# Staggering the starts of eight weight buffers by 64 bytes each

## The reference

```python
for l in range(DEPTH):
    h = rms_norm(x, pre_mix_g[l])
    mix = parallel_mixer(h, positions, w_in[l], ...)
    x = x + rms_norm(mix, post_mix_g[l])
    h = rms_norm(x, pre_cross_g[l])
    x = x + rms_norm(memory_cross_attention(h, mem_n, ...), post_cross_g[l])
    h = rms_norm(x, pre_ffn_g[l])
    x = x + rms_norm(swiglu(h, w_gate[l], w_up[l], w_down[l]), post_ffn_g[l])
```

## Time and profile before

| what | value |
|---|---|
| time, median of 3 runs | 2247.41 us |
| the three runs | 2243.59, 2257.13, 2247.41 us |
| span of the profiled execution | 2240.2 us |
| PE busy | 2145.6 us, 96% |
| DVE busy | 1403.7 us, 63% |
| ACT busy | 1127.0 us, 50% |
| POOL busy | 72.4 us, 3% |
| mean granted TensorE clock | 0.983 |

### The profile page before, as it was taken

One profiled execution on the slowest core, in us unless ns is written; L12 is line 12 of the kernel. 1 busy time (PEld: TensorE's weight loads), 2 busy tenths in 40 slices (PEclk: granted clock), 3 DMA queues, 4 the chain that ended last, 5 costly groups with the idle time before them and its releaser, 6 DMA issues.

```text
span 2240.2 us, 40831 instructions
## 1 busy us (share of the span) xinstructions
PE 2145.6 (96%) x17446; PEld 2047.7 (91%) x17446; DVE 1403.7 (63%) x2152; ACT 1127.0 (50%) x1757; POOL 72.4 (3%) x80
## 2 busy tenths in 40 slices
PE   7979999999989999999999999999999999999999
PEld 6868899989868899999998888999999998889999
DVE  5755566656646566566568667665666666668664
ACT  4554444444735444454546555545444456556443
POOL 4100000000000000000000000000000000000000
PEclk9989999999989999999999999999999989999999
DMA  6433346746415265645655224566566553335654
GB/s 216 151 113 104 106 150 212 217 145 194 135 51 167 90 190 196 205 163 191 205 186 171 95 95 142 184 192 205 180 195 203 174 170 114 95 114 168 198 195 155
DMA packets 98485, 360.33 MB, mean 161 GB/s; under 512 B 11136, under 2 KB 11149, under 8 KB 97920
## 3 DMA queue, kind: packets, MB, share of 16 engines
q1 hardware_dynamic: 96192, 349.22, 47.8%
q0 software_dynamic: 1680, 5.35, 0.8%
q10 hardware_dynamic: 432, 3.15, 0.4%
HBM read 356.61 MB, written 3.43 MB: 161 GB/s over the span
## 4 chain that ended last, share of the span: by engine, by line
PE 81%; DVE 12%; ACT 5%; issue 1%; DMA 0%; DVEq 0%; ACTq 0%; SPq 0%
PE bank L296 71%; DVE w_lo L1437 3%; PE bank L408 2%; ACT w_hi L907 1%; DVE rinv L1828 1%; PE bank L413 1%; PE bank L409 1%; PE bank L322 1%; DVE xn_lo L1459 1%; PE bank L759 1%; DVE sq L1499 1%; DVE x L1503 1%; DVE sq L2015 1%; DVE scale L1477 0%; DMA raw<-in_stream 0%
## 5 line engine op out<-in xcount | busy, mean ns | idle before, releaser
L1437 DVE TENSOR_TENSOR w_lo<-raw,w_hi 128x1024 fp32r<-128x1024 f32 x664 | 793.8, 1232 | 381.2 <-ACT w_hi L907 380.8
L296 PE MATMUL bank<-xn_hi,w_hi 128*128 128x256 f32 x3168 | 892.2, 282 | 38.3 <-DVE xn_lo L1459 30.2
L296 PE MATMUL bank<-xn_lo,w_hi 128*128 128x256 f32 x3168 | 880.5, 278 | 0.0
L296 PE MATMUL bank<-xn_hi,w_lo 128*128 128x256 f32 x3168 | 880.4, 278 | 0.0
L907 ACT ACTIVATE w_hi<-raw 128x1024 fp32r<-128x1024 f32 x664 | 672.2, 1050 | 231.6 <-PE bank L296 209.9
L296 PEld LDWEIGHTS bank<-xn_hi,w_hi 128*128 128x128 f32 x3168 | 598.4, 189 | 51.2 <-issue 25.8
L296 PEld LDWEIGHTS bank<-xn_lo,w_hi 128*128 128x128 f32 x3168 | 598.4, 189 | 1.3 <-issue 1.0
L296 PEld LDWEIGHTS bank<-xn_hi,w_lo 128*128 128x128 f32 x3168 | 598.0, 189 | 0.0
L296 PE MATMUL bank<-hid_hi,w_lo 128*128 128x256 f32 x1056 | 291.5, 276 | 0.0
L296 PE MATMUL bank<-hid_hi,w_hi 128*128 128x256 f32 x1056 | 291.5, 276 | 0.0
L296 PE MATMUL bank<-hid_lo,w_hi 128*128 128x256 f32 x1056 | 291.5, 276 | 0.0
(11 more groups left out here) (354 smaller groups left out, 2758.1 us busy)
## 6 DMA issues: line engine op xcount, KB each, us to landing
raw<-in_stream SPq DMA_DIRECT2D x664, 512.0 KB, 4.2
skew<-vec POOLq DMA_DIRECT2D x12, 192.0 KB, 4.2
table<-skew POOLq DMA_DIRECT2D x1, 1408.0 KB, 7.2
con<-in_con ACTq DMA_DIRECT2D x1, 1029.0 KB, 15.0
x<-in_x ACTq DMA_DIRECT2D x1, 1024.0 KB, 6.8
xn<-in_mem ACTq DMA_DIRECT2D x1, 1024.0 KB, 11.5
out<-x SPq DMA_DIRECT2D x4, 256.0 KB, 3.4
logit<-in_small POOLq DMA_DIRECT2D x3, 288.5 KB, 3.1
```

Source lines behind the costliest of these rows:

```text
L296: m = T.matmul(out, a, b, start=first and j == 0, stop=True, skip_group_check=True)
L1437: V.tensor_tensor(w_lo[m % RING], raw[m % RING], w_hi[m % RING].bitcast(F32), ALU.subtract).then_inc(*lo_done.next())
```

## The change

The buffers of `raw` stay where they are. Between each two of the eight buffers of `w_hi` and `w_lo` lies a new unused tile of 64 bytes, seven in all.

```diff
-    w_hi = [sb(f"w_hi{r}", [P, HK, COLS], F32R) for r in range(RING)]
-    w_lo = [sb(f"w_lo{r}", [P, HK, COLS], F32R) for r in range(RING)]
+    w_hi, w_lo = [], []
+    for part, ring in (("hi", w_hi), ("lo", w_lo)):
+        for r in range(RING):
+            if ring or part == "lo":
+                sb(f"offset_{part}{r}", [P, 16])
+            ring.append(sb(f"w_{part}{r}", [P, HK, COLS], F32R))
```

## The result

The changed kernel took 2285.7 us in the median of four runs (2283.99 to 2287.09), the kernel before 2251.14 us in its four. The ratio is 1.0168, with a 95% interval of 1.0131 to 1.0205. The forecast was no change at 2247 us; the time lies inside the stated range and in the case that had a chance of 0.25.

The account below looks back on a forecast made before the run. TensorE, busy 96% of the span, was taken as the bound, with matmul pitch the large lever. All five parts summed to 0, so the 2240.2 us span plus 7.2 us carried to the median gave 2247 us, range 2222 to 2298.

Parts of the forecast that it names:

- the case that had a chance of 0.25: The slow matmul pitch spreads through the feed-forward stretches: 2270 to 2298 us, chance 0.25.
- Part one: TensorE's matmul pitch: address distance alone does not set it, so taken as 0, bounds -13.6 to +50.7 us.
- The slower rival: Weights' load beside streamed activation read: a distance of 0 spreads the slow pitch, +50.7 us, 2298 us; chance 0.25.
- The faster rival: TensorE's two reads: stagger removes a standing clash, pitch falls to 109.2 ns, 73 us saved, 2174 us; chance 0.18.
- The case that the change does nothing: Unused tiles in the allocation could be dropped or padded away; called unlikely, time 2247 us, within the 0.57 for no effect.
- Parts two to five: w_lo on VectorE, w_hi on ScalarE, loads into raw, and tiles behind the rings moved by 448 bytes: each taken as 0.

Follow-up runs that it names:

- e1: Against the kernel before, only the tiles behind the rings moved up by 448 bytes, all weight buffers staying at byte 192: 2246.75 us, ratio 0.9994.
- e3: Against e1, all four w_lo buffers moved to byte 448, 256 from their w_hi, without a stagger: 2247.11 us, ratio 0.999 to before.
- e5: Against e1, everything from the shared area on, activations and weight buffers alike, moved 448 bytes higher: two runs, 2230.01 and 2265.8 us.
- e13: Against e1, only raw moved, to byte 256, weights staying at distance 64 from the activations: 2246.64 us, ratio 0.9971 to before.
- e7_both_128: Against e1, all w_hi and w_lo buffers moved to byte 256, distance 128 from the activations: 2301.07 us.
- e2_both_512: Against e1, all eight weight buffers moved to byte 640, distance 512 from the activations, no stagger: 2312.44 us, ratio 1.0294 to before.

## Why the prediction was wrong

**Part one, the matmul pitch, is the step that failed**, and nearly all of the 44.5 us with it. I took 0 where it was +42.9 us in the networks. The reason given was that four distances (64, 576, -64 and 448 bytes modulo 1 KB) "allow the fast pitch". Modulo 256 these are 64, 64, 192 and 192: two values, and the only two of the ten tried at which the fast pitch was found. The closing sentence named this hole, "a pitch that depends on the distance in a way that four distances happen to miss", and the range was wide enough for it, but the chance was set by the count of four. The change took w_hi to 64, 128, 192 and 256. The uniform kernels have 113.3 or 117.8, 118.7 or 120.0, 117.8, and 120.0 there; the changed kernel's four places have 113.6 or 117.9, 118.2 to 118.7, 117.7 to 117.9, and 119.6 to 120.3. So each place has nearly the pitch of its own distance, and the pitch of a network is their mean, 118.5 or 117.5.

The inference "one distance allows both pitches, so the address alone does not set it" was true and was used for too much. The old layout has both: over the five profiled kernels in which every weight buffer lies at 64 modulo 256 (before, `e1`, `e3`, `e5`, `e13`), 11 of 30 networks were slow. That is one part of the spread of the runs of before, 2230 to 2272 us over all sets. By the records' starts these five profiles lost about 15, 32, 23, 34 and 31 us to pitches above 113.3 ns, at spans of 2240.2, 2246.6, 2245.7, 2264.5 and 2250.7 us. The granted clock outside the networks is another part: `e1` and `e5` lost about as much to the pitch, at a mean clock of 0.989 and 0.982, and their spans are 17.9 us apart. Of the experiments' runs of before, the six with a clock of 0.987 or more took 2230 to 2245 us, the seven with 0.979 or less 2246 to 2267. At the other distances but 192 the pitch of 113.3 was not found. That the profile of before had six fast networks of six was luck, and its evenness looked like firmness.

**The slower rival** had the right place (the weights' load beside the streamed read), the right side and nearly the size: 50.7 us forecast for the fast stretches' going to 117.7, and 44.5 measured between the profiled spans, 37.8 by the ratio of the runs. Its trigger was wrong. It supposed one bad distance, 0, and a stream that stays slow after it. In `e7_both_128` no distance of 0 occurs and the loss is larger; and in the changed kernel's faster networks place 0 returns to 113.6 in each round of the ring, right after a place at 120.3. So a slow place does not drag the next one with it; each pays its own. Sticky is something else: which set of values a network has, 113.6 or 117.9 in place 0, holds from its second or third slot to its end.

**The faster rival** is refuted as far as tried: ten distances, none below 113.3 ns over a network. The gap to the 109.2 of bf16 stays unexplained. **The case that the change does nothing** is out.

**Parts two to five** held: w_lo 1221 against 1219 ns, w_hi 1045 against 1046, no new DMA share, and the moved tail at 0.9994.

**The rule of the Trainium skill** ("SBUF — State Buffer", section "Who interferes with whom") that gives TensorE two independent read ports and knows no contention but that of VectorE and GpSimd does not hold in its consequence: by it the sum was 0, and here moving nothing but the start of the weights moved the pitch between 113.3 and 120.0 ns (`e1_tail_only` against `e2_both_512`). The measurement decides.

**What stays open.** What repeats each 256 bytes is not known; the runs show only that the pitch does, at 0, 256 and 512, and where single buffers move by 256. Why a stretch at distance 64 settles at 113.3 or at 117.8 was not found. Inside a network's long unbroken stretch of 1,487 or 1,535 matmuls it never changed in the five profiles; short stretches ahead of it can have the other one. And why 64 with 0 mixed gives 122.2 stays open, as said there.

## What to carry to other kernels

Where TensorE is the bound and its pitch is above that of other matmuls of the same shape (here 109.2 ns in bf16), the start of the stationary operand relative to the streamed one is a parameter worth a sweep, modulo 256 bytes in the case here. A stagger between the buffers of one ring gives each buffer another distance, so they can't all have the best one, unless its step is a multiple of that period. Before counting observations as independent support, reduce them by every period that could be at work. And one profile in which all networks agree does not tell that their pitch is firm: the second pitch in its mixers and the spread of the runs were the hints.

## What was not expected of the hardware

- The pitch of the split fp32 matmuls (128x128 weights, 256 columns) at full granted clock takes values from 113.3 to 122.2 ns by the start of the stationary operand less that of the streamed one, modulo 256 bytes, 7.9% between best and worst. With w_hi and w_lo at one distance it goes up to 120.0.
- Where activations and weights swap roles, the pitch is that of the negative distance: 116.6 ns for 32, as for 224; 120.0 for 96, as for 160.
- The values 113.3 and 120.0 ns are 272 and 288 cycles of 2.4 GHz, 16 apart. 117.8 ns is no mixture of the two: in the second network of `e1_tail_only` all steps from one start to the next are 116 to 120 ns. The 118.7 ns of `e7_both_128` is a mixture, of steps of 115 to 122 ns.
- VectorE and ScalarE don't care: w_lo had a median of 1219 to 1222 ns and w_hi one of 1045 to 1049 in all twenty profiled kernels, with raw, w_hi and w_lo at equal and at different starts.
